# Cross-attention over a memory: the product of probabilities and values as three fp32r products of split operands instead of one f32 product

## The reference, cut to what matters

```python
def memory_xattn(h, mem, mem_g, wq, wkv, wo, q_g, k_g):
    q = rmsnorm((h @ wq).reshape(B, S, X_HEADS, X_HD), q_g)      # 4 heads of 256
    kv = (m @ wkv).reshape(B, m.shape[1], 2, X_HEADS, X_HD)
    k, v = rmsnorm(kv[:, :, 0], k_g), kv[:, :, 1]
    s = jnp.einsum('bshd,bmhd->bhsm', q, k) * (X_HD ** -0.5)
    p = jax.nn.softmax(s, axis=-1)
    o = jnp.einsum('bhsm,bmhd->bshd', p, v)
    return o.reshape(B, S, X_HEADS * X_HD) @ wo
```

## Time and profile before

| | us |
|---|---|
| Median of 3 runs (lowest, highest) | 1582.98 (1580.68, 1586.64) |
| The profiled execution's own time | 1583.1 |
| Its span, first to last instruction | 1581.4 |
| PE busy | 1442.3 (91% of the span) |
| DVE busy | 976.8 (62%) |
| ACT busy | 769.7 (49%) |
| Mean granted TensorE clock | 0.958 of 2.4 GHz |

### The profile page before, as it was taken

The page is one execution under the profiler, slowest core; times in us unless marked ns, Lnnn a source line. Parts: engine busy times, 40 slices in busy tenths (PEclk is TensorE's granted clock), DMA queues, the critical chain, the costliest instruction groups (busy, mean ns, idle before and its releaser), DMA issues. The chain is left out here.

```text
span 1581.4 us, 19686 instructions
## 1 busy us (share of the span) xinstructions
PE 1442.3 (91%) x7753; PEld 1213.4 (77%) x7753; DVE 976.8 (62%) x1301; ACT 769.7 (49%) x1126; POOL 144.6 (9%) x159
## 2 busy tenths in 40 slices
PE   6999899979999996999996899999999896999993
PEld 5787677767787675999994688887887585999982
DVE  4474658575554526999984522554255446999974
ACT  3322555475333524877763425322144435777760
POOL 1000001100000000313211000000000002122210
PEclk9999999979999997999998899999999997999997
DMA  6823111123522065899985432222421165899965
GB/s 193 146 59 109 56 54 54 40 92 118 195 80 80 1 230 192 311 370 382 369 333 200 148 103 80 84 76 98 159 81 53 44 231 213 335 368 381 383 243 212
DMA packets 111006, 274.98 MB, mean 174 GB/s; under 512 B 41777, under 2 KB 44226, under 8 KB 106306
## 3 DMA queue, kind: packets, MB, share of 16 engines
q1 hardware_dynamic: 95506, 203.96, 37.3%
q10 hardware_dynamic: 5904, 52.96, 8.5%
q0 software_dynamic: 9504, 16.80, 2.8%
HBM read 266.27 MB, written 25.17 MB: 184 GB/s over the span
## 5 line engine op out<-in xcount | busy, mean ns | idle before, releaser
L185 DVE TENSOR_TENSOR w_lo<-w_stage,w_hi 128x2048 fp32r<-128x2048 f32 (+2 forms) x32 | 67.2, 2103 | 187.7 <-ACT w_hi L175 177.6
L175 ACT ACTIVATE w_hi<-w_stage 128x2048 fp32r<-128x2048 f32 (+2 forms) x34 | 60.2, 1773 | 235.5 <-PE bank L240 153.4
L200 DVE TENSOR_TENSOR w_lo<-w_stage,w_hi 128x2048 fp32r<-128x2048 f32 x42 | 96.1, 2289 | 58.6 <-ACT w_hi L194 33.8
L194 ACT ACTIVATE w_hi<-w_stage 128x2048 fp32r<-128x2048 f32 x40 | 76.6, 1914 | 96.2 <-PE bank L240 59.6
L2934 PE MATMUL bank<-e_wi_lo,e_hx_hi 128*128 128x384 f32 x256 | 86.7, 338 | 0.0
L2933 PE MATMUL bank<-e_wi_lo,e_hx_hi 128*128 128x384 f32 x256 | 86.6, 338 | 0.0
L240 PE MATMUL bank<-w_hi,h_sg_hi 128*128 128x512 f32 x192 | 76.6, 399 | 4.4 <-DVE h_sg_lo L2360 2.1
L2792 POOL DMA_INDIRECT e_tok<-moe_h,moe_slots x32 | 67.8, 2119 | 113.4 <-issue 88.1
L2788 DVE TENSOR_TENSOR e_wi_lo<-e_room,w_hi 128x1536 fp32r<-128x1536 f32 x40 | 68.6, 1752 | 12.2 <-ACT w_hi L2784 11.4
L240 PE MATMUL bank<-w_hi,h_sg_lo 128*128 128x512 f32 x192 | 75.3, 392 | 0.0
L240 PE MATMUL bank<-w_lo,h_sg_hi 128*128 128x512 f32 x192 | 75.2, 392 | 0.0
(11 more groups left out here) (544 smaller groups left out, 4159.3 us busy)
## 6 DMA issues: line engine op xcount, KB each, us to landing
e_room<-in_moe_w_in SPq DMA_DIRECT2D x88, 768.0 KB, 9.5
w_stage<-in_moe_w_in SPq DMA_DIRECT2D x40, 768.0 KB, 8.1
e_wo<-in_moe_w_out ACTq DMA_DIRECT2D x16, 1536.0 KB, 10.8
e_room<-in_moe_w_out ACTq DMA_DIRECT2D x14, 1536.0 KB, 10.8
w_stage<-in_x_wkv SPq DMA_DIRECT2D x16, 1024.0 KB, 5.1
w_stage<-in_sg_w_in SPq DMA_DIRECT2D x16, 1024.0 KB, 5.4
w_stage<-in_hyb_w_in SPq DMA_DIRECT2D x10, 1024.0 KB, 5.1
w_stage<-in_x_wq SPq DMA_DIRECT2D x8, 1024.0 KB, 5.0
```

The costliest lines, as they stand in the source:

```text
L175: act.activation(self.w_hi[h][:, :, :cols], self.stage[h][:, :, :cols], ACT.Copy)\
L185: dve.tensor_tensor(self.w_lo[h][:, :, :cols], self.stage[h][:, :, :cols], self.w_hi[h][:, :, :cols], ALU.subtract).then_inc(self.lo_done[ ...
L194: act.activation(self.w_hi[h][:, :, :cols], self.stage[h][:, :, :cols], ACT.Copy).then_inc(self.hi_done[h], 1)
L200: engine.tensor_tensor(self.w_lo[h][:, :, :cols], self.stage[h][:, :, :cols], self.w_hi[h][:, :, :cols], ALU.subtract).then_inc(self.lo_do ...
```

## The change

The values product is computed in three fp32r terms. The values are split in `into_queries`, by a new class `MemoryParts`: the high part by one ACTIVATE over 128x2048 elements after `keep_norm(3)`, the low part by one TENSOR_TENSOR over 128x2048 after `half_lo(first_q, 1)`. The parts lie in a buffer of the mixer phase that is no longer used (`spare`), and `cross_attend` keeps that place free with an unused tile. The wait for the values and keys that come back from DRAM in layer 1 moves from PE's list in `cross_attend` to ACT's list in `into_queries`. In `cross_attend` ACT's copy of T(u) goes to `pT_hi` in fp32r, DVE forms `pT_lo` by a subtraction from PSUM (`turned_lo`), and it is now this subtraction that raises `kept`, for which V(h) and T(u+2) wait. For each d and j three fp32r products of 512 columns stand where one f32 product stood. The edits that only pass the new object along are cut:

```diff
+class MemoryParts:
+    def __init__(self, kT, v, spare):
+        a, b = spare
+        self.kT, self.v = kT, v
+        self.whole = v
+        self.hi, self.lo = (b[:, 4 * e:4 * e + 4, :].rearrange("p (j a) n -> p j (a n)", j=MT) for e in range(2))
+    def begin(self, m, name):
+        self.hi_made, self.lo_made = m.psem(f"{name}_mem_hi"), m.psem(f"{name}_mem_lo")
+    def split_hi(self, act):
+        act.activation(self.hi, self.whole[:, :, :], ACT.Copy).then_inc(self.hi_made, 1)
+    def split_lo(self, dve):
+        dve.wait_ge(self.hi_made, 1)
+        dve.tensor_tensor(self.lo, self.whole[:, :, :], self.hi, ALU.subtract).then_inc(self.lo_made, 1)
...
@@ into_queries, ACT @@
                 m.half_hi(act, first_q, 1)
                 keep_norm(3)
+                res.wait(act, T - 1)
+                if back is not None:
+                    act.wait_ge(back[0].back, 32)
+                memory.split_hi(act)
                 m.half_hi(act, first_q + 1, 0)
@@ into_queries, DVE @@
                 m.half_lo(dve, first_q, 1)
+                memory.split_lo(dve)
                 m.half_lo(dve, first_q + 1, 0)
@@ cross_attend @@
+        m.sb(t, f"{name}_parts_room", [P, 2 * KD, S], side=room_side)
         prob = m.sb(t, f"{name}_prob", [P, RING, 2, N_MEM])
-        pT = m.sb(t, f"{name}_pT", [P, 2, MT, S])
+        pT_hi, pT_lo = (m.sb(t, f"{name}_pT_{s}", [P, 2, MT, S], F32R) for s in ("hi", "lo"))
@@ cross_attend, PE @@
-                if back is not None:
-                    pe.wait_ge(back, 32)
...
+                            cols = slice(h * XHD + d * P, h * XHD + (d + 1) * P)
                             for j in range(MT):
-                                ins = pe.matmul(out_ps[d][:, :], v[:, j, h * XHD + d * P:h * XHD + (d + 1) * P],
-                                                pT[:, h % 2, j, :], start=j == 0, stop=j == MT - 1)
+                                for term, (x, y) in enumerate(((memory.hi, pT_hi), (memory.lo, pT_hi), (memory.hi, pT_lo))):
+                                    ins = pe.matmul(out_ps[d][:, :], x[:, j, cols], y[:, h % 2, j, :],
+                                                    start=j == 0 and term == 0, stop=j == MT - 1 and term == 2)
@@ cross_attend, ACT @@
-                    act.activation(pT[:, h % 2, :, i * P:(i + 2) * P],
-                                   turn_ps[u % 2][:, :].rearrange("p (j t) -> p j t", j=MT), ACT.Copy).then_inc(kept, 1)
+                    act.activation(pT_hi[:, h % 2, :, i * P:(i + 2) * P],
+                                   turn_ps[u % 2][:, :].rearrange("p (j t) -> p j t", j=MT), ACT.Copy).then_inc(p_hi_out, 1)
@@ cross_attend, DVE @@
+                def turned_lo(u):
+                    h, i = units[u]
+                    dve.wait_ge(p_hi_out, u + 1)
+                    rows = slice(i * P, (i + 2) * P)
+                    dve.tensor_tensor(pT_lo[:, h % 2, :, rows], turn_ps[u % 2][:, :].rearrange("p (j t) -> p j t", j=MT),
+                                      pT_hi[:, h % 2, :, rows], ALU.subtract).then_inc(kept, 1)
                 for u, (h, i) in enumerate(units):
                     if u + 1 < NU:
                         normalize(u + 1)
                     if u + AHEAD < NU:
                         maximum(u + AHEAD)
+                    turned_lo(u)
                     if h and i == 0:
                         rest(h - 1)
```

More of the change, by code:

```diff
@@ L1784, in turn, with into_queries @@
         ins.then_inc(self.turned, 1)
-def into_queries(m, layer, first, parts, first_q, qT, qn, xn, x_in=None, mix=None, back=None):
+class MemoryParts:
[11 more added lines that the diff above has]
+        dve.tensor_tensor(self.lo, self.whole[:, :, :], self.hi, ALU.subtract).then_inc(self.lo_made, 1)
+def into_queries(m, layer, first, parts, first_q, qT, qn, xn, memory, x_in=None, mix=None, back=None):
     m.phase()
@@ L1806, in into_queries @@
                                           "out_dve", "normed", "q_turned", "kept_act", "kept_dve", "m_turned", "m_hi", "m_lo"))
+        memory.begin(m, nm)
         def q_bank(n, b):
@@ L2018, in hybrid_layer, with cross_attend @@
         pair = m.split_pair(c, "mixT")
-        into_queries(m, 0, first + 7 + 4 * DEPTH, [pair], first + 9 + 4 * DEPTH, qT, qn, xn, x_in=m.sem("x_again"),
+        parts = MemoryParts(kv.kT[0], kv.v[0], pair)
+        into_queries(m, 0, first + 7 + 4 * DEPTH, [pair], first + 9 + 4 * DEPTH, qT, qn, xn, parts, x_in=m.sem("x_again"),
                      mix=MixParts(kv, (nsa_mix, gla_mix)))
         right[1].close()
-    return qT, qn
-def cross_attend(m, name, qT, qn, kT, v, o_hi, o_lo, back=None):
+    return qT, qn, parts
+def cross_attend(m, name, qT, qn, memory, o_hi, o_lo, room_side):
     m.phase()
@@ L2038, in cross_attend @@
                                         "dve", "q_turned", "q_act", "q_dve"))
+    p_hi_out = m.psem(f"{name}_p_hi_out")
     with ExitStack() as t:
+        m.sb(t, f"{name}_parts_room", [P, 2 * KD, S], side=room_side)
         prob = m.sb(t, f"{name}_prob", [P, RING, 2, N_MEM])
-        pT = m.sb(t, f"{name}_pT", [P, 2, MT, S])
+        pT_hi, pT_lo = (m.sb(t, f"{name}_pT_{s}", [P, 2, MT, S], F32R) for s in ("hi", "lo"))
+        kT = memory.kT
         nmax = m.sb(t, f"{name}_nmax", [P, NU, 2])
@@ L2451, in sgu_layer @@
     qn = m.sb(cq, "x1_qn", [P, T, GC])
+    parts = MemoryParts(kT, v, (lo, hi))
     um_ctx.close()
@@ L2456, in sgu_layer @@
     into_queries(m, layer, first + 2 * NGR, gated_parts,
-                 first + 2 * NGR + 4, qT, qn, xn, back=(kv, kT, v))
+                 first + 2 * NGR + 4, qT, qn, xn, parts, back=(kv, kT, v))
     um_ctx.close()
-    return qT, qn, kT, v
+    return qT, qn, parts
 class Routing:
@@ L3275, in build_trunk @@
                 if layer == 0:
-                    (qT, qn), kT, v = hybrid_layer(m, at["hyb"], kv, right, cq), kv.kT[0], kv.v[0]
+                    qT, qn, parts = hybrid_layer(m, at["hyb"], kv, right, cq)
                 else:
-                    qT, qn, kT, v = sgu_layer(m, layer, at["sgu"], kv, cq, combine)
+                    qT, qn, parts = sgu_layer(m, layer, at["sgu"], kv, cq, combine)
                 o_ctx = ExitStack()
                 o = m.split_pair(o_ctx, f"x{layer}_o", side="right")
-                cross_attend(m, f"x{layer}_at", qT, qn, kT, v, *o, kv.back if layer else None)
+                cross_attend(m, f"x{layer}_at", qT, qn, parts, *o, "right" if layer else None)
             if layer == 0:
```

## The result

The kernel after takes 1610.39 us in the median of 4 runs (1604.25 to 1611.47), the kernel before 1581.90 in the median of the 4 beside it. The ratio is 1.0163 with a 95% interval of 1.0145 to 1.0182, some 26 us more by the ratio; the two medians lie 28.5 apart. The profiled execution took 1610.19 us against 1583.1, +27.1, and its span is 1608.4 us.

What follows compares the result with a forecast made beforehand. Bound: the loop between PE and helper engines in `cross_attend`, where a helper's list, now DVE's, makes V wait. Waits of 14.2 us and clock falls of 6.8 on 1583.1 give 1604 us; range 1595 to 1613.

Steps and rivals of the forecast that it cites:

- the clock falls more often or for longer: Rival: in `cross_attend` falls also before V(3), or for two stretches each; 1609 to 1614 us, chance 0.12.
- The product, 12 steps of 0.227 and 0.10: V on PE: 12 fp32r matmuls take 2.83 us where f32 took 3.54, saving 0.71 us per head.
- Head 0, V(0) late by 1.62: V(0) waits for DVE's low part of T(1), behind normalization and maximum: 1.62 us later per layer.
- The cycle of 11.93 in heads 1 and 2: V(0) to V(1) and V(1) to V(2), set by DVE's list: 11.93 us, before 9.01 and 8.99.
- Head 3's 6.64: V(2) to V(3), with no weight half in the list: 6.64 us where it was 6.30, +0.34.
- +7.1 us per layer without the clock: Sum of `cross_attend`'s waits less the shorter last product, at full clock: +7.1 us per layer, +14.2 for two.
- The splits of the values cost 0: In `into_queries` both splits fit idle gaps of ACT and DVE: cost 0, DVE keeping 1.15 us of slack.
- The clock: two falls per layer at 1.7 us, 3.4: One fall of PE's clock at each long pause, before V(1) and V(2): 1.7 us each, +6.8 in all.
- The mean clock of the phase, 0.85: Sign: PEclk's mean over `cross_attend` falls to 0.85 or so.
- the same waits but the clock holds: Rival: the waits in `cross_attend` cost +14.2 us with no added clock falls; 1597.3 us, chance 0.18.
- PE's own pace: Rival: DVE's low part is done when V's turn comes, so the phase shortens by 5.7 us; 1577.4, chance 0.03.
- three signs of being wrong: DVE idle right before the low part in heads 1 and 2; V(h) 3.5 us at full clock; `into_queries` longer.

Runs made afterwards that it cites:

- run 3: Changed kernel with PE's pauses before V(1), V(2) and V(3) filled by 18, 18 and 10 unread fp32r products; 1598.24 us.
- run 2: Changed kernel with the f32 product back, V still waiting for DVE's subtraction, whose result nothing reads; 1611.66 us.
- run 4: Changed kernel with DVE's weight half moved behind the low part, to units 3 and 5 from 2 and 4; 1593.95 us.
- run 5: Changed kernel with DVE's low part ahead of normalization and maximum at each head's second unit; 1597.46 us.
- run 1: Changed kernel with `cross_attend` put back as before; value splits, reserved place and moved wait stay; 1581.35 us, 0.9986 of the kernel before.
- run 9: Changed kernel with low-part terms last, weight halves at units 3 and 5 on ACT and DVE, remaining PE pauses filled with unread products; 1574.46 us.
- run 7: Changed kernel with low-part terms last and weight halves at units 3 and 5 on ACT and DVE; 1583.33 us, 1.0003 of the kernel before.
- run 8: Kernel before, f32 product, with weight halves at units 3 and 5 on ACT and DVE; 1580.86 us, ratio 0.9989.

## Why the prediction was right, and where it was short

The time, 1610.39, lies in the range of 1595 to 1613, the sign and the cause are those forecast, and it is 6 us above the value given, outside the 1600 to 1608 that had the chance of 0.55. What came is the last rival, "the clock falls more often or for longer" (1609 to 1614, chance 0.12), with both of its conditions at once: a fall before V(3) too, and each as long as two stretches. The waits were forecast to within 0.3 us per layer, by run 3; the clock was not. One of the four executions took 1604.25 us at a mean clock of 0.954 where the others had 0.945 to 0.947, so the falls are not the same in each; the steps here are those of the profiled one, in layer 0:

- *The product, 12 steps of 0.227 and 0.10.* Held where the clock was up: 2.90 for V(0), 2.86 in run 3.
- *Head 0, V(0) late by 1.62.* 13.19 us behind the phase's start where it was 11.67: 1.52. In layer 1 it is 13.25 against 11.60, 1.65.
- *The cycle of 11.93 in heads 1 and 2.* V(0) to V(1) took 12.00, and the pause was 4.61 where 4.6 was forecast. Run 3's layer 1 gives 11.95 and 11.97, runs 2, 4 and 5 change it by what they add to or take from DVE's list. Head 3's 6.64 is 6.66 in run 3.
- *+7.1 us per layer without the clock.* Shown by run 3's layer 1: +7.4, with V(0) 1.8 us late in place of 1.62.
- *The splits of the values cost 0.* Shown by run 1, with the forecast slack of 1.15.
- *The clock: two falls per layer at 1.7 us, 3.4.* **This is the term that was mis-sized.** There were three falls per layer, not two (the pause before V(3), 2.77 us, was enough), and each was 6.83 us long, not 3.41. V(1) to V(2) took 14.39 where 11.93 is the cycle at full clock, V(2) to V(3) 8.77 against 6.64, V(3) to the next phase 7.17 against 4.67: 2.5 + 2.1 + 2.5 = 7.1 us per layer. I had priced a fall by the one at the phase's start, behind which PE was busy at once. Here the low stretch began while PE still waited, went on through a V that is all on the path, and so cost 2.1 to 2.5 us, nearly all that halving V's pace costs (5.29 - 2.86 = 2.43). Over two layers that is 14.2 in place of 6.8. The 7.4 between them, less the 1.5 us by which the rest of the kernel was shorter in this execution, are the 6 us by which the forecast was low. The upper end that the prediction gave for this term, about 16, covers it; that the rest came out 1.5 us shorter was luck and had no part in the forecast.
- *The mean clock of the phase, 0.85.* It is 0.79, for the same reason.

Of the rivals, "the same waits but the clock holds" is what run 3 is, at 1598.24 where 1597.3 was worked out. PE's own pace never set the time of V(1) to V(3) in the changed kernel. In run 9 PE's pauses before V(0), V(1) and V(2) are 0.16 us, and the fp32r product wins there 2.3 us in the two phases, of the 5.7 that the count of products promised; the waits of head 3 are still there, under the filling.

None of the three signs of being wrong came: DVE has no idle time right before the low part in heads 1 and 2, V takes 2.9 us with the clock up, and `into_queries` kept its length.

The Trainium skill, FP8 and Floating Point Precision, TensorE Precision Notes, has four passes for true FP32, and the estimate worked out from that was a saving of 0.91 us per head. At full clock V takes 3.54 us in f32 and 2.86 to 2.90 in fp32r, so 0.64 to 0.68 is saved: the row's 0.71 is near and 0.91 is not. The number of passes is not refuted by this: an f32 product takes 0.86 us, which is four times 0.215, and it is the fp32r product that takes more than that, 0.227.

The Trainium skill, TensorE: Matmul & The Clock Gate, section on HAM oscillation, has each burst behind a long wait start at half rate, in a kernel with waits of some 3 to 5 us. The trace of after agrees: behind 6 pauses of 2.8 to 4.6 us there are 6 falls, two of them behind pauses shorter than those of that kernel. Run 5's layer 1 doesn't: it has two pauses of 3.21 us and no fall.

## What to carry to other kernels

Before an operand is split on a helper engine, count what stands in that engine's list between the producer and the split, not how busy the engine is: here DVE was idle for 45% of the phase before the change, but not in the stretch in which the new wait falls. If a sum has terms that need only the first part, put them first and let them wait for that part alone: here that gave back 26 us of the loss. Where a change makes PE's pauses longer, add the clock to the price of the wait, up to the time of the whole burst behind it at half speed, and test it by filling the pause with unread products: here that alone gave back 12 us. No safe length of a pause comes out of these runs: two of 3.21 us passed without a fall in one layer of run 5, and 1.37 and 0.69 us in run 7 did not.

## What was not expected of the hardware

- A pause need not be long: in run 7 the clock fell behind pauses of 1.37 and 0.69 us, in both layers. A quicker product may thus bring its own penalty.
- The same list with the same pauses (3.21 us, run 5) has three falls in one layer and none in the other, 5.5 us apart. A single execution of such a kernel doesn't tell its time: run 5's four range from 1595.52 to 1602.77. The kernel before ranges as widely, from 1580.06 to 1587.31 in the 29 beside it.
- PE's 2.9 us between two phases have a price in the kernel before too. With 10 unread products there and a later weight half it is 0.48% faster, 0.11% of it by the weight half alone (run 8).
